# Last attention of a two-block kernel: v first and turned between units, the causal mask added by TensorE, the two maps combined in one step

## The reference, cut to what matters

```python
def diff_attention(h, w_qkv, w_o, ..., subln_g, lambda_init):
    q, k, v = jnp.split(h @ w_qkv, 3, axis=-1)      # q, k: 8 heads x 2 maps x 64; v: 8 heads x 128
    lam = exp(sum(lq1 * lk1)) - exp(sum(lq2 * lk2)) + lambda_init
    # per block of 128 queries:
    s = jnp.einsum('bqhcd,bkhcd->bhcqk', qi, k) * (d ** -0.5)
    p = jax.nn.softmax(jnp.where(key_pos <= qpos, s, neg), axis=-1)
    a = p[:, :, 0] - lam * p[:, :, 1]
    o = jnp.einsum('bhqk,bkhe->bqhe', a, v)
    o = rmsnorm(o, subln_g) * (1.0 - lambda_init)   # over the 128 columns of each head
    return o.reshape(bsz, L, H * 2 * d) @ w_o
```

## Time and profile before

| | us |
|---|---|
| median of 3 runs | 1770.26 (1769.58 to 1773.39) |
| profiled execution: span from first to last instruction | 1768.6 |
| mean granted TensorE clock in it | 0.932 of 2.4 GHz |
| last unit of qkv ends | 1461.5 |
| last output product of the attention ends | 1518.2 |
| first matmul of w_o | 1527.9 |

### The profile page before, as it was taken

One profiled execution on the slowest core, in us unless ns is written; L12 is line 12 of the kernel. 1 busy time (PEld: TensorE's weight loads), 2 busy tenths in 40 slices (PEclk: granted clock), 3 DMA queues, 4 the chain that ended last, 5 costly groups with the idle time before them and its releaser, 6 DMA issues.

```text
span 1768.6 us, 30284 instructions
## 1 busy us (share of the span) xinstructions
PE 1598.4 (90%) x12312; PEld 1543.1 (87%) x12312; DVE 1061.1 (60%) x1273; ACT 760.4 (43%) x1008; POOL 6.4 (0%) x21
## 2 busy tenths in 40 slices
PE   6869999989899998999954999979999798879997
PEld 5848999987799997999954999979999796779996
DVE  7774665558756545666457666466653656476653
ACT  4233554341645534444435434343444336454442
POOL 0000000001000000000000000000000000000000
PEclk9957999999999999999986999989999896789998
DMA  7600556642236665456630656635566351146671
GB/s 181 164 16 25 165 184 178 187 140 74 71 118 191 181 179 164 145 181 189 179 92 23 187 169 193 179 104 168 184 187 174 107 179 49 41 126 190 190 205 57
DMA packets 346672, 252.63 MB, mean 143 GB/s; under 512 B 32574, under 2 KB 345820, under 8 KB 346604
## 3 DMA queue, kind: packets, MB, share of 16 engines
q1 hardware_dynamic: 345136, 250.00, 47.7%
q10 hardware_dynamic: 1468, 1.69, 0.3%
HBM read 250.63 MB, written 1.05 MB: 142 GB/s over the span
## 4 chain that ended last, share of the span: by engine, by line
PE 83%; DVE 11%; ACT 4%; issue 1%; DMA 1%; ACTq 0%; DVEq 0%; SPq 0%
PE acc L447 25%; PE acc L448 25%; PE acc L449 25%; PE acc L593 3%; PE spare L571 2%; DVE w_low L1258 2%; PE acc L579 2%; ACT w_high L860 1%; DVE x_state L1448 1%; DVE evac_a L1446 1%; DVE xg_low L1302 1%; PE spare L457 1%; DVE squares L1287 1%; DMA w_raw<-in_ffn_w_dram 0%; PE spare L493 0%
## 5 line engine op out<-in xcount | busy, mean ns | idle before, releaser
L447 PE MATMUL acc<-xg_high,w_high 128*128 128x272 f32 (+4 forms) x2608 | 757.6, 290 | 74.7 <-DVE xg_low L1302 45.5
L1258 DVE TENSOR_TENSOR w_low<-w_raw,w_high 128x2048 fp32r<-128x2048 f32 (+3 forms) x229 | 540.7, 2361 | 421.0 <-ACT w_high L860 420.7
L448 PE MATMUL acc<-xg_low,w_high 128*128 128x272 f32 (+4 forms) x2608 | 750.6, 288 | 0.0
L449 PE MATMUL acc<-xg_high,w_low 128*128 128x272 f32 (+4 forms) x2608 | 747.7, 287 | 0.0
L860 ACT ACTIVATE w_high<-w_raw 128x2048 fp32r<-128x2048 f32 (+3 forms) x229 | 451.5, 1971 | 684.8 <-PE acc L449 668.0
L447 PEld LDWEIGHTS acc<-xg_high,w_high 128*128 128x128 f32 (+3 forms) x2608 | 497.4, 191 | 85.9 <-issue 76.2
L448 PEld LDWEIGHTS acc<-xg_low,w_high 128*128 128x128 f32 (+3 forms) x2608 | 496.2, 190 | 4.3 <-issue 3.7
L449 PEld LDWEIGHTS acc<-xg_high,w_low 128*128 128x128 f32 (+3 forms) x2608 | 496.1, 190 | 0.2
L447 PE MATMUL acc<-hidden_high,w_high 128*128 128x256 f32 (+1 forms) x1216 | 347.0, 285 | 1.8 <-DVE w_low L1258 1.8
L449 PE MATMUL acc<-hidden_high,w_low 128*128 128x256 f32 (+1 forms) x1216 | 346.5, 285 | 0.0
L448 PE MATMUL acc<-hidden_low,w_high 128*128 128x256 f32 (+1 forms) x1216 | 345.5, 284 | 0.0
(11 more groups left out here) (173 smaller groups left out, 1011.6 us busy)
## 6 DMA issues: line engine op xcount, KB each, us to landing
w_raw<-in_ffn_w_dram SPq DMA_DIRECT2D x88, 1024.0 KB, 5.3
w_raw<-in_ffn_w_dram SPq DMA_DIRECT2D x32, 1408.0 KB, 7.1
w_raw<-in_mlp_w_up_dram SPq DMA_DIRECT2D x32, 1024.0 KB, 5.4
w_raw<-in_mlp_w_down_dram SPq DMA_DIRECT2D x32, 1024.0 KB, 5.8
w_raw<-in_attn_w_qkv_dram SPq DMA_DIRECT2D x12, 1024.0 KB, 5.2
w_raw<-in_a_w_in_dram SPq DMA_DIRECT2D x18, 256.0 KB, 4.5
w_raw<-in_a_w_in_dram SPq DMA_DIRECT2D x4, 1024.0 KB, 7.5
w_raw<-in_a_w_out_dram SPq DMA_DIRECT2D x4, 1024.0 KB, 5.1
```

The source lines that it names most:

```text
L447: pe.matmul(dst, high_w, high, start=first, stop=False)
L448: pe.matmul(dst, high_w, low, start=False, stop=False)
L449: return pe.matmul(dst, low_w, high, start=False, stop=last)
L1258: dve.tensor_tensor(wlo[c % 2][:, s], raw[c % 2][:, s], whi[c % 2][:, s].bitcast(F32), ALU.subtract)\
```

## The change

- **Order of qkv.** The chunks are loaded as v, k, q. After each of units 4 to 9 PE does four of the 24 transposes of v (the last two groups are the 16 leftover tokens), and ACT copies them. The scores of pieces 0 and 1 stand ahead of unit 11, which is the last of q (heads 6 and 7).
- **Order of pieces.** All eight heads of block 0 (144 keys), then all eight of block 1 (272 keys).
- **Mask on PE.** The scale goes into q (`rstd2`). After each map's score matmul PE adds the causal mask of the 128 diagonal keys with a matmul of the identity (128 rows) by the mask. DVE's pass L1531 falls away; DVE takes the maxima and ACT the exponentials straight out of the accumulator.
- **One-step combination.** The map is a - b * (lambda * sum_a / sum_b), one instruction over the keys where there were two; 1/sum_a is applied by ACT when it takes the output (`keep_out`).
- **PT on DVE.** The copies of the transposed map go from ACT to DVE (`turned`).
- **Moved split.** The high and low parts of the second w_o chunk (`split(g.c0 + 13)`) stood right after unit 11 and now stand at step 4 of the attention, on both ACT and DVE.
- **Tail.** 1/rms and the multiplication of block 0 are done at steps 11 to 13; after the last piece only block 1 is left, in two halves, and PE turns block 0 meanwhile.

```diff
@@ tensor
+            pieces = [(i, h) for i in range(2) for h in range(DIFF_HEADS)]
+            before = 2 * len(pieces)
+            def turn_values(q):
+                i, half = q // 2, q % 2
+                nt = META if i == 2 else P
+                pe.wait_ge(S["dve_evac"], g.r0 + 4)
+                if q >= 4:
+                    pe.wait_ge(S["v_ready"], n.get("v_ready") + q - 3)
+                for m in range(4):
+                    ins = pe.transpose(sp[i % 2][0:nt, half, m * P:(m + 1) * P],
+                                       vF[:, 4 * half + m, i * P:i * P + nt], ident)
+                ins.then_inc(S["v_turned"], 1)
+            def make_scores(p):
+                i, h = pieces[p]
+                nk, d0 = (i + 1) * P + META, i * P + META
+                if p >= 2:
+                    pe.wait_ge(S["exp_done"], before + p - 1)
+                for c in range(2):
+                    r = slice(c * HD, (c + 1) * HD)
+                    pe.matmul(sp[p % 2][:, c, 0:nk], qC[r, h, i * P:(i + 1) * P], kC[r, h, 0:nk], start=True, stop=False)
+                    ins = pe.matmul(sp[p % 2][:, c, d0:nk], ident, cst[:, C_CAUSAL + META:C_CAUSAL + META + P],
+                                    start=False, stop=True)
+                ins.then_inc(S["s_full"], 1)
...
+            for j in range(1, 11):
                 wide(g, j, 0, T2)
-            turn_v(g, 8, [(0, P), (P, P), (2 * P, META)])
+                if 4 <= j < 10:
+                    turn_values(j - 4)
+            pe.wait_ge(S["v_ready"], n.add("v_ready", 6))
+            pe.wait_ge(S["dve_evac"], g.r0 + 9)
+            make_scores(0)
+            make_scores(1)
+            wide(g, 11, 0, T2)
             begin(G["w_o"])
+            for p in range(N + 2):
+                if 2 <= p + 1 < N and p:
+                    make_scores(p + 1)
+                if 1 <= p <= N:
+                    turn_probs(p - 1)
+                if p >= 2:
+                    make_out(p - 2)
@@ scalar
+            for p in range(N + 3):
+                if p < N:
+                    exps(p)
+                if p == 4:
+                    split(g.c0 + 13)
+                if p >= 3:
+                    keep_out(p - 3)
+                if p == 12:
+                    out_guess(0)
@@ vector
+            row_max(0)
+            row_max(1)
+            difference(0)
+            take(11)
+            N = len(pieces)
+            for p in range(1, N + 2):
+                if 2 <= p < N:
+                    row_max(p)
+                if 2 <= p <= N:
+                    difference(p - 1)
+                if p >= 2:
+                    turned(p - 2)
+                if p == 4:
+                    split(g.c0 + 13)
+                if p == 11:
+                    out_variance(0)
+                if p == 13:
+                    dve.wait_ge(S["c_guess"], 1)
+                    newton(rsC[:, 0], guC[:, 0], vaC[:, 0], stC[:, 0])
+                    out_normed(0, 0, DIFF_HEADS)
...
+            out_variance(1)
+            dve.wait_ge(S["c_guess"], 2)
+            newton(rsC[:, 1], guC[:, 1], vaC[:, 1], stC[:, 1])
+            out_normed(1, 0, 4)
+            out_normed(1, 4, DIFF_HEADS)
             out_low(GAIN["attn_subln_2"])
```

More of the change, by code:

```diff
@@ L236, in two_blocks_kernel @@
         rowinv = place("row_inverse", [P, 4, 2])
+        rowmix = place("row_mix", [P, 4])
         region = cursor[0]
@@ L409, in _ @@
             ffn(2)
-            straight("qkv", A["attn_w_qkv_2"][0], 256)
+            w = rows(A["attn_w_qkv_2"][0])
+            for j in range(12):
+                col = 256 * (j % 4) + D * (2 - j // 4)
+                load_chunk(G["qkv"].c0 + j, w[:, :, col:col + 256])
             straight("w_o", A["attn_w_o_2"][0], 256)
@@ L806, in _ @@
             sum_squares(T2, 1)
-            for j in range(1, 12):
-                wide(g, j, 0, T2)
-            turn_v(g, 8, [(0, P), (P, P), (2 * P, META)])
-            begin(G["w_o"])
[L811 to L816, removed]
@@ L817, in _ @@
-            turn_out("o_all", 1)
+            pieces = [(i, h) for i in range(2) for h in range(DIFF_HEADS)]
[10 more added lines that the diff above has]
+                ins.then_inc(S["v_turned"], 1)
@@ new lines, in prob_tiles, with turn_probs @@
+            def prob_tiles(i):
+                return [(k * P, P) for k in range(i + 1)] + [((i + 1) * P, META)]
+            def turn_probs(p):
+                pe.wait_ge(S["probs_ready"], p + 1)
+                if p >= 2:
+                    pe.wait_ge(S["pt_ready"], before + p - 1)
+                for slot, (k0, nk) in enumerate(prob_tiles(pieces[p][0])):
+                    ins = pe.transpose(acc[0][0:nk, p % 2, slot * P:(slot + 1) * P], Pr[p % 2][:, 0, k0:k0 + nk], ident)
+                ins.then_inc(S["pt_full"], 1)
@@ new lines, in make_out @@
+            def make_out(p):
+                i, h = pieces[p]
+                pe.wait_ge(S["pt_ready"], before + p + 1)
+                if p >= 2:
+                    pe.wait_ge(S["o_read"], before + p - 1)
+                for slot, (k0, nk) in enumerate(prob_tiles(i)):
+                    ins = pe.matmul(acc[1][:, p % 2, 0:P], PT[p % 2][0:nk, slot, :], vC[0:nk, slot, h * P:(h + 1) * P],
+                                    start=slot == 0, stop=slot == i + 1)
+                ins.then_inc(S["o_full"], 1)
@@ new lines, in _ @@
+            for j in range(1, 11):
+                wide(g, j, 0, T2)
+                if 4 <= j < 10:
[5 more added lines that the diff above has]
+            wide(g, 11, 0, T2)
+            begin(G["w_o"])
+            N = len(pieces)
[4 more added lines that the diff above has]
+                    turn_probs(p - 1)
+                if p >= 2:
+                    make_out(p - 2)
@@ new lines, in _ @@
+            for i in range(2):
+                for half in range(2):
+                    pe.wait_ge(S["o_all"], 1 if i == 0 else 2 + half)
+                    if i == 0:
+                        pe.wait_ge(S["exp_done"], before + N)
+                    for k in range(4):
+                        ins = pe.transpose(sp[i][:, half, k * P:(k + 1) * P],
+                                           O[:, i, (4 * half + k) * P:(4 * half + k + 1) * P], ident)
+                    ins.then_inc(S["o_turned"], 1)
@@ L1198, in _ @@
             root(T2)
-            for j in range(12):
-                split(g.c0 + j + 2)
[L1201 to L1218, removed]
+            pieces = [(i, h) for i in range(2) for h in range(DIFF_HEADS)]
+            before = 2 * len(pieces)
+            def exps(p):
+                act.wait_ge(S["s_read"], before + p + 1)
+                if p >= 2:
+                    act.wait_ge(S["pt_full"], before + p - 1)
+                nk = (pieces[p][0] + 1) * P + META
+                for c in range(2):
+                    ins = act.activation(Pr[p % 2][:, c, 0:nk], sp[p % 2][:, c, 0:nk], ACT.Exp,
+                                         bias=rowneg[:, p % 4, c:c + 1], accum_out=rowsum[:, p % 4, c:c + 1])
+                ins.then_inc(S["exp_done"], 1)
@@ new lines, in keep_out @@
+            def keep_out(p):
+                i, h = pieces[p]
+                act.wait_ge(S["o_full"], before + p + 1)
+                if p:
+                    act.wait_ge(S["o_read"], before + p)
+                act.activation(O[:, i, h * P:(h + 1) * P], acc[1][:, p % 2, 0:P], ACT.Identity,
+                               scale=rowinv[:, p % 4, 0:1])
+                act.activation(ta[0][:, 0, 0:P], acc[1][:, p % 2, 0:P], ACT.Square, scale=rowinv[:, p % 4, 0:1],
+                               accum_out=ssC[:, i, h:h + 1]).then_inc(S["o_read"], 1)
@@ new lines, in out_guess @@
+            def out_guess(i):
+                act.wait_ge(S["c_var"], i + 1)
+                link(act.activation(guC[:, i], vaC[:, i], ACT.Ln))
+                act.activation(guC[:, i], guC[:, i], ACT.Exp, scale=-0.5).then_inc(S["c_guess"], 1)
+            for j in range(11):
+                split(g.c0 + j + 2)
+                if 4 <= j < 10:
+                    i, h = (j - 4) // 2, j % 2
+                    nt = META if i == 2 else P
+                    act.wait_ge(S["v_turned"], n.add("v_turned"))
+                    act.activation(vC[0:nt, i, h * 512:(h + 1) * 512], sp[i % 2][0:nt, h, :], ACT.Copy)\
+                        .then_inc(S["v_ready"], 1)
@@ L1219, in _ @@
+            N = len(pieces)
+            for p in range(N + 3):
[7 more added lines that the diff above has]
+                    out_guess(0)
+            n.add("s_read", N)
+            n.add("pt_full", N)
+            n.add("o_full", N)
+            out_guess(1)
             out_high(GAIN["attn_subln_2"])
@@ L1800, in _, with take @@
             refine(rstd, T2)
-            for j in range(12):
-                u = g.u0 + j
+            link(dve.tensor_scalar(rstd2[:, META:T2], rstd[:, META:T2], DIFF_SCALE, None, ALU.mult))
+            def take(j):
+                m = 2 * (j % 4)
```

(52 more changed lines are left out.)

## The result

The changed kernel takes 1790.74 us (median of 4, 1789.66 to 1792.88); the kernel before, beside it, 1769.92 (4 runs). The medians differ by 20.8 us; the recorded ratio, which is not simply that of the two medians, is 1.0107, interval 1.009 to 1.0125, or 19 us. 1790.0 was forecast, 19.8 more than before. The profiled execution spans 1787.9 us against 1768.6.

What follows compares the result with a forecast made beforehand. PE's work and its clock were taken to bound the kernel. Attention +22.9, late fall of the clock -1.5, tail -3.1 and w_o's start +1.5 gave +19.8, 1790.0 us; range 1766 to 1800, the main case's own 1781 to 1799.

Steps and rivals of the forecast that it cites:

- The price of the mask: PE, last attention: four more records and two more changeovers a piece; a pair 10.6 us against 6.16 at 1.2 GHz.
- the changeover: PE going over to another set of rows: 0.295 us at 1.2 GHz, taken as 0.20 at 2.4 GHz.
- The stop: Step 4 of the attention: the moved split delays piece 4's map, so PE stands still 1.8 to 2.0 us.
- The clock: Last attention: falls at PE's gap with pieces 0 to 3 done, then 0.50 to the end; forecast's chance 0.69.
- The sum: From unit 10's end to the last output: 6.2 before unit 11 ends, 73.4 after; 79.6 against 56.7, +22.9 us.
- the late fall of the clock: After the gap at step 4 begins, the clock falls somewhat later, not at once: -1.5 us.
- The tail: Last output to w_o: half the multiplication done early, block 0's transposes hidden; 6.5 in place of 9.6, -3.1 us.
- The start of w_o: After the tail: w_o's first 3 us at 1.2 GHz, +1.5 us (0 to 2.4).
- the split transposes: Tail: 16 transposes in a row, split 8 and 8, may not bring the clock back to 1.00 before w_o.
- The sum of all: Whole kernel: +22.9 - 1.5 - 3.1 + 1.5 = +19.8, 1790.0 us.
- The clock holds: Rival, last attention: PE's gap at step 4 does not drop the clock; -5.4, 1764.9 us, chance 0.13.
- It comes back with the large pieces: Rival, last attention: the clock falls and returns with the large pieces; 22 of the loss goes, 1768 us, chance 0.08.

Runs made afterwards that it cites:

- the split in quarters: Changed kernel with the second w_o chunk's split in quarters, ACT at steps 3 to 6, DVE at 8 to 11: 1762.21 us, ratio 0.9933.
- The fillers: Changed kernel with seven unread matmuls of the identity by the mask ahead of piece 4's transposes: 1765.81 us, ratio 0.9963.
- both edits: Changed kernel with the split in quarters and the matmul order score, score, mask, mask: 1751.87 us, ratio 0.9881.

## Why the prediction was right

Step by step, the changed kernel's trace beside the working:

- **The price of the mask.** Right in every term: score blocks 3.84 for large pieces, outputs 1.15 and 1.57, transposes 0.43 and 0.64 at 1.2 GHz (0.83 only for the last two pieces, which have no scores ahead of them). At 2.4 GHz the one value without a row, the changeover, was put at 0.20 between bounds of 0.10 and 0.295: the score block of a small piece took 0.44 + 0.42 + 0.44 + 0.42 = 1.72 for 1.71, and in the split in quarters that of a large one 2.14 for 2.14. The mask alone in the kernel before gave 10.64 a pair for 10.6. The Trainium skill, TensorEngine Tiling (Array Packing), Key Properties, has it that a change of tiling mode drains the engine; 0.295 and 0.20 us at each change of rows are in keeping with that, though no run shows that the time is a drain.
- **The stop.** Its chain was right, its length 1.5 us (1.8 to 2.0 forecast): ACT's and DVE's five steps took 6.6 us together, not 6.9, and PE's two rounds the 5.1 of the forecast.
- **The clock.** It fell there and stayed down to the tail. The fillers show that PE's idleness was the cause, the quarters that without it the same mix mostly keeps 1.00. The Trainium skill, TensorE: Matmul & The Clock Gate, Part 1, warns of long waits between bursts of matmuls, and, under "A second HAM failure mode", of a kernel in which PE's short idles between groups of matmuls came often enough to bring the clock down. The longest idle here was 1.50 us, shorter than the waits of its first case, and the clock fell; this trace is nearer to its second.
- **The sum.** From the end of unit 11 to the last output 72.3, where the sum has 73.4 less 1.5 for the late fall of the clock, 71.9. The two terms ahead of it were transposes 2.64 for 2.8 (six times 0.44) and scores 3.43 for 3.4.
- **The tail.** 6.4 for 6.5, and that is partly luck, for the chain was another. I had DVE's two halves of the multiplication and then four low parts, 1.25 + 3.2. At 0.50 it ran from the first half through PE's transposes of block 1 and one high and one low part:

```profile
1540.43 0.70 DVE attn_out L1958
1541.18 1.98 PE spare L886 x8
1543.18 0.70 ACT xg_high L1147
1543.91 0.76 DVE xg_low L1671
```

At 1.00, in the traces of the split in quarters and of both edits, the chain is the forecast one, 1.29 for the two halves and 2.65 for the four low parts, and the tail is 6.1.
- **The start of w_o.** It cost 2.6 us (25.3 against 22.7), where I had 1.5 with bounds of 0 and 2.4: this term was mis-sized, and lies outside its bounds. The clock was at 0.50 for the first 5.5 us of w_o, not 3. The reason I gave, the split transposes, is not shown: with the sixteen in one run w_o started at 0.50 too in two traces of three, so the fast start in the profiled execution of before was in part its luck.
- **The sum of all** is 2.64 + 3.43 + 72.3 - 56.7 = 21.7, less 3.2 in the tail, plus 2.6: 21.1; the spans differ by 19.3, since qkv up to unit 11 and the stages around it took 1.8 us less in this execution.
- **The rivals.** "The clock holds" was put at 1764.9; with the stop filled it is 1765.8, and with the stop removed 1762.2. As a price it was right: 47.9 us after unit 11 with the stop filled, for 48.4. It left out that w_o starts at 0.50 in these versions too (24.7 us for 22.7 in the split in quarters). "It comes back with the large pieces" I gave 0.08 because no slow attention had done so; in the order score, score, mask, mask it does. For the changed kernel it did not.

The lesson of the two directions: the change lengthens PE's part at 1.2 GHz by 4.5 us a pair and takes away waits at the opening and 3 us of the tail. With the clock it is a gain of 6 to 12 us (ratios 0.9963 and 0.9933), without it a loss of 20; the 1.5 us for which the moved split leaves PE idle decide which.

## What to carry to other kernels

When PE is the bound of a thin mix of small matmuls, price the mix at both levels of the clock, and look for the first place where it stands idle: here a conversion of 4.2 us, moved into the middle of a pipeline, cost 25 us by way of the clock. Such work is better cut into pieces that fit into the slack of each step. Count the changes between matmuls of 64, 16 and 128 rows: putting the two half-array matmuls next to each other and the full ones behind them, with the same instructions, was worth 31 us here (1790.7 to 1759.4; part of it because the clock came back), and with the split in quarters gave the best version, 1.2% under the kernel before.

## What the runs showed that I had not expected

- Seven matmuls whose results are unread made the kernel 25 us faster (1790.7 to 1765.8), by keeping the clock through 1.5 us.
- One program can end either way: with the split in quarters, eight executions of ten took 1752 to 1767 us and two 1787.
- The clock was regained inside an attention (0.51 to 0.99 at 1498.8) by nothing but the order of the four matmuls of a piece. PE had been busy for all of the 20.4 us before; in the changed kernel it was busy for all of 56.2 us and the clock stayed at 0.50.
- The same tail starts w_o at either level of the clock: at 1.00 in the kernel before, at 0.50 in two versions whose tail is the same.
- Executions of a kernel differ by several us ahead of the attention: unit 11 ended at 1464.1 and at 1470.1 us in two versions that are the same up to there.
